# A three-mixer block with its input norm applied after the projections, and its bias table moved in pieces

## What is computed

```python
def rms_norm(x, w):
    y = x32 * lax.rsqrt(jnp.mean(x32 * x32, axis=-1, keepdims=True) + EPS)
    return (y * w.astype(f32)).astype(x.dtype)
...
h = rms_norm(x, norm1_w[l])
cols = split_cols(h @ w_in[l], IN_SIZES)
...
y_a = short_conv_mixer(a_b, a_c, a_u, conv_w[l], conv_b[l])    # b * (conv(c * u) + bias)
y_b = nsa_mixer(...)     # compressed, selected and window attention, with bias_w = rel_bias[t5_bucket(dist)]
y_c = mla_mixer(...)
y_d = stick_breaking_mixer(...)
x = x + rms_norm(y, ...) @ w_out[l]
```

## Time and profile before

| | |
|---|---|
| device time, three runs | 1957.11, 1959.37, 1961.04 us (median 1959.37) |
| span of the profiled execution | 1953.4 us |
| busy: PE / DVE / ACT / POOL | 1843.6 (94%) / 885.3 (45%) / 425.1 (22%) / 1018.2 (52%) us |
| weight slots | 284 of 512 KB, 3.3 us from issue to landing (median) |
| TensorE's granted clock, mean of the span | 0.970 of full |

### The profile page before, as it was taken

One profiled execution on the slowest core, in us unless ns is written; L12 is line 12 of the kernel. 1 busy time (PEld: TensorE's weight loads), 2 busy tenths in 40 slices (PEclk: granted clock), 3 DMA queues, 4 the chain that ended last, 5 costly groups with the idle time before them and its releaser, 6 DMA issues.

```text
span 1953.4 us, 21963 instructions
## 1 busy us (share of the span) xinstructions
PE 1843.6 (94%) x8480; PEld 1442.8 (74%) x8480; DVE 885.3 (45%) x1372; ACT 425.1 (22%) x910; POOL 1018.2 (52%) x584
## 2 busy tenths in 40 slices
PE   6699889999999999999999999999999899999996
PEld 4485556788888886777887778677778668888885
DVE  5236864664036322435004365666655654304434
ACT  1214565121012101222003132455400210000001
POOL 3492110566666665455664444444466646666664
PEclk8899999999999999999999889999999999999998
DMA  4441010222222223122322112311122212222221
GB/s 158 150 149 48 23 44 22 87 94 96 98 95 97 96 93 108 65 75 76 106 96 76 65 55 67 115 61 65 63 89 95 86 55 97 97 97 97 97 97 54
DMA packets 48526, 166.38 MB, mean 85 GB/s; under 512 B 5531, under 2 KB 6875, under 8 KB 48040
## 3 DMA queue, kind: packets, MB, share of 16 engines
q1 hardware_dynamic: 45596, 159.77, 24.4%
q10 hardware_dynamic: 2828, 5.21, 0.9%
HBM read 161.98 MB, written 3.94 MB: 85 GB/s over the span
## 4 chain that ended last, share of the span: by engine, by line
PE 79%; DVE 9%; POOL 3%; ACT 3%; issue 3%; DMA 3%; SPq 1%; DVEq 0%; ACTq 0%; POOLq 0%
PE bank L652 78%; DMA w_raw<-in_w 2%; POOL w_lo_t L1889 2%; DVE tmp L1404 2%; POOL w_hi_t L1887 1%; PE bank L910 1%; DVE o_hi L1382 1%; DVE o_lo L1383 1%; DVE att_l_t L1672 0%; DMA x_sb<-in_x 0%; ACT L1065 0%; DVE h_lo L1450 0%; ACT rstd_t L1114 0%; DVE att_l_t L1813 0%; SPq L1911 0%
## 5 line engine op out<-in xcount | busy, mean ns | idle before, releaser
L1887 POOL TENSOR_SCALAR w_hi_t<-w_raw 128x1024 fp32r<-128x1024 f32 x284 | 307.5, 1083 | 887.3 <-PE bank L652 835.3
L1889 POOL TENSOR_TENSOR w_lo_t<-w_raw,w_hi_t 128x1024 fp32r<-128x1024 f32 x284 | 693.1, 2440 | 23.7
L652 PE MATMUL bank<-h_hi,w_hi_t 128*128 128x512 f32 x1344 | 546.9, 407 | 25.8 <-POOL w_lo_t L1889 14.4
L652 PE MATMUL bank<-h_lo,w_hi_t 128*128 128x512 f32 x1344 | 531.0, 395 | 0.6 <-DVE h_lo L1450 0.5
L652 PE MATMUL bank<-h_hi,w_lo_t 128*128 128x512 f32 x1344 | 530.0, 394 | 0.0
L652 PEld LDWEIGHTS bank<-h_hi,w_hi_t 128*128 128x128 f32 x1344 | 256.6, 191 | 103.4 <-issue 31.1
L652 PEld LDWEIGHTS bank<-h_lo,w_hi_t 128*128 128x128 f32 x1344 | 256.9, 191 | 56.7 <-DVE h_lo L1450 3.6
L652 PEld LDWEIGHTS bank<-h_hi,w_lo_t 128*128 128x128 f32 x1344 | 256.5, 191 | 55.4 <-issue 0.2
L652 PE MATMUL bank<-hid_hi,w_lo_t 128*128 128x512 f32 x432 | 168.1, 389 | 0.0
L652 PE MATMUL bank<-hid_hi,w_hi_t 128*128 128x512 f32 x432 | 168.0, 389 | 0.0
L652 PE MATMUL bank<-hid_lo,w_hi_t 128*128 128x512 f32 x432 | 168.0, 389 | 0.0
(11 more groups left out here) (253 smaller groups left out, 2262.5 us busy)
## 6 DMA issues: line engine op xcount, KB each, us to landing
w_raw<-in_w SPq DMA_DIRECT2D x284, 512.0 KB, 3.3
x_sb<-in_x SPq DMA_DIRECT2D x4, 512.0 KB, 6.6
x_sb<-in_x ACTq DMA_DIRECT2D x2, 1024.0 KB, 5.6
alibi<-in_alibi SPq DMA_DIRECT2D x8, 256.0 KB, 5.9
out_y<-x_sb SPq DMA_DIRECT2D x8, 256.0 KB, 2.0
scratch<-table SPq DMA_DIRECT2D x1, 1280.0 KB
toep<-scratch SPq DMA_DIRECT2D x4, 256.0 KB
decay<-in_decay SPq DMA_DIRECT2D x1, 1024.0 KB, 4.9
```

The source lines that it names most:

```text
L652: return pe.matmul(out, lhs, rhs, start=start, stop=stop, **kw)
L1887: pool.tensor_scalar(hi, raw, 1.0, 0.0, ALU.mult, ALU.add).then_inc(*did("w_hi", i))
L1889: pool.tensor_tensor(lo, raw, hi.bitcast(F32), ALU.subtract).then_inc(*did("w_lo", i))
```

## The change

The factor r is kept in a buffer of its own, `r_h`, and is no longer in h: h_hi = rounded x * w (ACT, a new step "u"), h_lo = x * w - h_hi (DVE, one instruction of three operands). PE starts with kvc and ksw, two projections together, up to the last chunk but one; then the norm's sums, then the last chunk. nq0 follows on its own. Each evacuation multiplies by r_h on DVE; v1, which has positions on partitions, is scaled on ACT by a column `r_col` that PE makes by four small matmuls (step `r_cols`). In the convolution, b, c and u each need r: c is multiplied by r_h twice (for u too), and the sum that b multiplies once.

SP loads the first two weight slots ahead of x. `ones` and `ones64` are made by memsets on DVE and not loaded. Six weights and two masks of the mixers are loaded by ACT later, next to projections. The bias table is made after nq0, leaves at n = 6, goes to the scratch area head by head (n = 8 to 11) and comes back head by head (n = 13 to 16). `onehot`, `tab`, `causal` and `kv_raw` take other places in SBUF.

```diff
-    run(sqs("n1", KD) + [("norm", "n1"), ("apply_h", "n1", "norm1"), ("bias_tables", 0)])
-    part, ends = together(("kvc", "ksw", "nq0"))
-    run([part(0, KD)] + ends)
+    for c in range(KD):
+        run([("u", "n1", c), ("sq", "n1", c)])
+    part, ends = together(("kvc", "ksw"))
+    run([part(0, KD - 1), ("norm", "n1"), part(KD - 1, KD)] + ends)
...
-    run([("sq", "ksw", 0), F("nq1"), ("sq", "nq0", 0), ("norm", "ksw"), ("cmp_x", 0), ("nsa_apply", "ksw"),
-         F("cq0"), ("sq", "nq1", 0), ("norm", "nq0"), ("cmp_x", 1), ("nsa_apply", "nq0"),
+    run([("sq", "ksw", 0), ("cmp_x", 0), F("nq0"), ("cmp_x", 1), ("bias_tables", 0), ("norm", "ksw"),
+         ("nsa_apply", "ksw"), F("nq1"), ("sq", "nq0", 0), F("cq0"), ("sq", "nq1", 0), ("norm", "nq0"),
+         ("nsa_apply", "nq0"),
...
-         U(1, 0), F("sk0"), U(1, 1), F("sk1"), U(1, 2), v1[0], U(1, 3), v1[1], v1[2],
+         U(1, 0), F("sk0"), ("r_cols", "n1"), U(1, 1), F("sk1"), U(1, 2), v1[0], U(1, 3), v1[1], v1[2],
...
+UNNORMED = ("n1",)
+FIRST_LOADS = 2
+TABLE_AT, SCRATCH_AT, BIAS_AT = 6, 8, 13
...
+            elif stage == "u":
+
+                _, key, c = step
+                srcs, waits = norms[key][0], norms[key][6]
+                wait_src(act, waits[c])
+                act.activation(h_hi[:, c], srcs[c], ACT.Copy, scale=col(U_WEIGHT[key], c))\
+                   .then_inc(*did("h_hi", key, c))
...
+            elif stage == "u":
+
+                _, key, c = step
+                own("h_hi", key, c)
+                dve.scalar_tensor_tensor(out=h_lo[:, c], in0=norms[key][0][c], scalar=col(U_WEIGHT[key], c),
+                                         in1=h_hi[:, c].bitcast(F32), op0=ALU.mult, op1=ALU.subtract)\
+                   .then_inc(*did("h_ready", key, c))
...
+                elif name in ("ksw", "nq0", "nq1", "cq0", "ckv", "sk0", "sk1"):
+                    dst = {"ksw": ks_d, "nq0": nq[:, 0], "nq1": nq[:, 1], "cq0": cq[:, 0], "ckv": ckv[:],
+                           "sk0": s_qk[:, 2], "sk1": s_qk[:, 3]}[name]
+                    dve.wait_ge(*full(name))
+                    dve.tensor_tensor(dst, ps(name)[:], r_h[:], ALU.mult).then_inc(*release(name))
...
-                        ins = dve.tensor_copy(conv_t[:, 1, 2:2 + T], ps(name)[:])
+                        chain(dve.tensor_tensor(conv_t[:, 1, 2:2 + T], ps(name)[:], r_h[:], ALU.mult))
+                        ins = dve.tensor_tensor(conv_t[:, 1, 2:2 + T], conv_t[:, 1, 2:2 + T], r_h[:], ALU.mult)
...
+                        chain(dve.tensor_tensor(yc, yc, r_h[:], ALU.mult))
                         ins = dve.tensor_tensor(conv_t[:, 1, 2:2 + T], ps(name)[:], yc, ALU.mult)
...
+        def rows_of(h):
+
+            sp.wait_ge(C.sem["table_out"], 16)
+            for k, (c0, w) in enumerate(((0, 640), (640, 1024))):
+                rows = P if k == 0 else N_CMP
+                dst = a["scratch"][h, k, 0:rows * w].rearrange("(p w) -> p w", w=w)
+                sp.dma_start(dst, a["table"][h:h + 1, c0:c0 + w].to_broadcast([rows, w]))\
+                  .then_inc(C.sem["bias_out0"], 16)
+
+        def bias_of(h):
+
+            sp.wait_ge(C.sem["bias_out0"], 16 * 2 * NH)
```

More of the change, by code:

```diff
@@ L358, in _program @@
     epst = sb("epst", [P, 8])
+    r_h = sb("r_h", [P, T])
+    r_col = sb("r_col", [P, NT])
     area = ExitStack()
@@ L405, in _program @@
     ckv = sp_("ckv", [P, T])
-    sp_("rest of onehot", [P, 640 + 1024 - 1536])
+    sp_("up to cb_t", [P, 640 + 1024 - 1536])
     mq = sp_("mq", [P, NH, T])
@@ L554, in _program @@
     norm_at = {k: i for i, k in enumerate(norm_order)}
+    ring_order = [k for k in norm_order if k not in UNNORMED]
+    ring_at = {k: i for i, k in enumerate(ring_order)}
     sq_use = {}
@@ L710, in _ @@
                 ms(step[1], len(norms[step[1]][0]))
+            elif stage == "r_cols":
+                key = step[1]
+                pe.wait_ge(*after("rstd", key))
+                out = take(("r_cols", key))
+                for t in range(NT):
+                    last = mm(out[:, t:t + 1], r_h[0:1, t * P:(t + 1) * P], ones[0:1, 0:1], True, True,
+                              skip_group_check=True)
+                fill(("r_cols", key), last)
             elif stage == "sq" and step[1] in PE_SUM:
@@ L1408, in _ @@
         ins.then_inc(*did("table", "eps"))
+        dve.memset(ones[:], 1.0).then_inc(*did("ones_set"))
+        chain(dve.memset(ones64[:], 0.0))
+        for g in range(2):
+            gs = slice(g * HD, (g + 1) * HD)
+            chain(dve.memset(ones64[gs, gs], 1.0))
         dve.memset(rb[N_BUCKETS:N_BUCKETS + 1, :], NEG).then_inc(*did("bcast_v"))
@@ L1894, in _ @@
     def _(sp):
+        for i in range(FIRST_LOADS):
+            sp.dma_start(w_raw[:, i], a["w"][i]).then_inc(C.sem[f"w_landed{i}"], 16)
         for g in range(4):
@@ L1897, in _ @@
         n = 0
-        def bias_tables(part):
-            if part == 0:
-                for nn in range(len(TAB)):
-                    sp.wait_ge(*evacuated(("tab", nn)))
-                sp.dma_start(a["table"], tab[:]).then_inc(C.sem["table_out"], 16)
-                return
-            if part == 1:
-                sp.wait_ge(C.sem["table_out"], 16)
-                for k, (c0, w) in enumerate(((0, 640), (640, 1024))):
-                    rows = P if k == 0 else N_CMP
-                    dst = a["scratch"][:, k, 0:rows * w].rearrange("h (p w) -> h p w", w=w)
-                    sp.dma_start(dst, a["table"][:, None, c0:c0 + w].to_broadcast([NH, rows, w]))\
-                      .then_inc(C.sem["bias_out0"], 16)
-                return
-            sp.wait_ge(C.sem["bias_out0"], 16 * 2)
-            t = a["scratch"].tensor
-            for h in range(NH):
-                sp.dma_start(toep[:, h], bass.AP(tensor=t, offset=(2 * h) * P * 1024 + P - 1,
-                                                 ap=[[640 - 1, P], [1, T]])).then_inc(C.sem["bias_in"], 16)
-                sp.dma_start(cb_t[:, h], bass.AP(tensor=t, offset=(2 * h + 1) * P * 1024 + T - CMP_LEN + 1,
-                                                 ap=[[1024 - CMP_STRIDE, N_CMP], [1, T]]))\
-                  .then_inc(C.sem["bias_in"], 16)
@@ new lines, in table_to_dram @@
+        def table_to_dram():
+            for nn in range(len(TAB)):
+                sp.wait_ge(*evacuated(("tab", nn)))
+            sp.dma_start(a["table"], tab[:]).then_inc(C.sem["table_out"], 16)
+        def rows_of(h):
[5 more added lines that the diff above has]
+                  .then_inc(C.sem["bias_out0"], 16)
```

128 lines of the change are left out of this document (77 added, 51 removed).

## The result

The changed kernel is slower: 1966.01 us median (1961.55 to 1967.24, 8 runs) against 1958.01 (1954.91 to 1961.04, 8 runs), a ratio of 1.0035, 95% interval 1.0024 to 1.0045. The forecast was 1953.8. The profiled execution has a span of 1965.0 us against 1953.4; these are 11.6 apart where the medians are 8.0 apart, because the profiled execution of the kernel before was its shortest run.

The account below looks back on a forecast made before the run. PE's matmuls were taken to bound the kernel, with only idle time before 151 us movable: 9.7 us gained at slot 16 minus 4.1 in the convolution, 5.6 off, gave 1953.8 us (own range 1950 to 1956.5; 8 in 10: 1934 to 1964).

Parts of the forecast that it names:

- the change touches none of those after the first mixer: PE's matmuls, nearly all of the 1953.4 us, stay untouched after the first mixer; only idle time before 151 us can move.
- The start: Up to the third weight slot: weights ahead of x, no wait for the norm; third slot done at 34.1, 9 us early.
- The bytes on one engine: Table to slot 16: scratch pieces, bias reads, weights and ACT's loads on one DMA engine at 25 GB/s, 52.3 us.
- the sum's 0.7 us of an idle engine: Ahead of slot 16: 0.7 us counted where the bias reads wait for the last scratch write.
- What waits beside POOL: DVE instructions reading two SBUF tensors wait while POOL works: 2.82 us beside it, 0.74 alone.
- The allowance of 3.4 us: First compress input on DVE: two-SBUF forms meet POOL's slot 5, up to 3.4 us more, making the table later.
- From span to time: Last step: median of the runs lies 6 us over the profiled span, so span 1947.8 becomes 1953.8 us.
- The rule for the rows: DMA copies: engines are the largest number up to 16 dividing the slowest dimension, so 31 rows run on one engine.
- The convolution's term: Four additional DVE multiplies by r_h in the convolution, on the chain: 4.1 us lost, between 1 and 6.
- Evacuations at nothing: Ten evacuation copies move from ACT to DVE multiplies of PSUM by r_h: taken as nothing, at most 10 x 0.1 us.
- Rival B: Slower: the queue stands at each of eight pieces; at 1.5 us each 12 us lost, 1966 us; chance 0.18.
- Rival A: Pieces nearly free: 31-row DRAM-to-DRAM copies spread, 1.1 us each; slot 16 at 91 to 93, 1936 us; chance 0.17.

Follow-up runs that it names:

- a_col: Changed kernel with r_col kept in unused columns of epst, so the working area starts at a multiple of 128 bytes again; 1954.3 us, ratio 0.9987 to before.
- b_pad: Kernel before with 32 unused bytes behind epst, so its working area starts at 32 modulo 64; 1966.41 us, ratio 1.0051.
- a_rows32: Changed kernel with 32 unused bytes behind r_col and its 31-row transfers made 32 rows; 1941.28 us, ratio 0.9914 to before.
- a_pad: Changed kernel with 32 unused bytes behind r_col, so the working area starts at 64 modulo 128; 1957.67 us, ratio 0.9997 to before.
- a_w32: Changed kernel with 32 unused bytes ahead of w_hi_t, so the split weights start at 32 modulo 64; 1977.2 us, ratio 1.0101 to before.

## Why the prediction was wrong

- **The step that failed** is the first paragraph's "the change touches none of those after the first mixer", and with it that nothing later is changed. The instructions and their order are the same there, but their operands' addresses are not: 9.4 us between the changed kernel and a_col, 10.0 between before and b_pad. None of the rivals held it. The 9.4 us are nearly the whole distance from the forecast's upper edge, 1956.5, to 1966.01.
- **The start was right.** First split 4.54 (5.5), slots 0 and 1 done at 11.8 (13.4), DVE's last h_lo at 22.95 (25.5), table copies at 46.1 (47.4), slot 16 at 109.0 (109.8), v1 9.9 us early (9.7). The bytes on one engine were right too, as the 32 rows show: from the table's landing to slot 16's 57.0 us (forecast 56.6). SyncE stood 8.5 us at the first bias read, but this isn't the sum's 0.7 us of an idle engine: the one engine worked on at 25 to 33 GB/s until the last scratch piece was written. That the sum met the trace within 1 us is in part luck, since it kept the one engine busy without a gap, and the chain has 11.3 us of POOL's splitting (82.79 to 94.07) between two loads.
- **What waits beside POOL** was drawn too narrowly, as instructions with two SBUF inputs. In the first compress input it was also a cast with one, 2.44 us beside POOL and 0.43 in the second input:

```profile
35.63 2.44 DVE L1408 CAST cmp_xh<-tmp 128x512 fp32r<-128x512 f32 x1
...
41.32 0.43 DVE L1408 CAST cmp_xh<-tmp 128x512 fp32r<-128x512 f32 x1
```

The allowance of 3.4 us held it all the same: that input took 6.1 us (32.72 to 38.81), forecast 2.8 + 3.4.
- **From span to time** the forecast added 6 us "for what lies around it". In the changed kernel's profiled run that is 1.8 us (1966.75 and 1965.0); the rest was that the profiled execution of before was the shortest of its runs. Against the eight runs' median of 1958.01, 5.6 us off would be 1952.4.
- **The rule for the rows.** The Trainium skill, "DMA: Bandwidth & Descriptors", section "Why a DMA increments its semaphore by 16 and not by 1", says that a copy runs on the largest number of engines up to 16 that divides the slowest dimension of both its sides. The trace agrees for a copy from DRAM to DRAM too: 25 GB/s with 31 rows, over 300 with 32.
- **The convolution's term was too small**: 4.1 against 4.7 to 5.3 in the traces up to 256 us and 6.1 to 9.2 in medians. (ac, 0) took 2.17 us, and the forecast had 1.9 to 2.1 for it. What is missing isn't shown; a lower clock behind PE's longer pauses would fit.
- **Evacuations at nothing** isn't contradicted: the 10 multiplies lie before v1, where the sum came out. No run tested it by itself.
- With the address put back (a_col) the change gives -2.5 us of the forecast -5.6, within 0.2% of the kernel before: 9.9 to 10.7 gained at the start, 5 to 9 given back by the four multiplies.
- Rival B named the right time, 1966, for a wrong reason: the start came out as forecast, and the issues of pieces take 1.2 us of the chain (48.45 to 49.73), where B needed 12. Rival A wasn't this kernel, but it is a_rows32: 16.2 us for it, where A had 17.8 more than the forecast.

## What to carry to other kernels

When a change adds, drops or resizes a tensor, compare the start addresses of all matmul operands before and after, and keep them at multiples of 128 bytes, which was the fastest of the starts tried here; a tensor of 16 bytes below a working area cost this kernel 0.5%. A group whose mean grows by a few ns in a stage that the diff doesn't touch, at full clock and 100% busy, is the mark of it. Give transfers a row count that divides over the engines even if the last row is waste, and fold a factor into an instruction that is there anyway before adding one on the chain.

## What the runs showed of the hardware

- Back-to-back fp32r matmuls of 512 columns start every 226.7 ns if both operands start at a multiple of 128 bytes in the partition (before, a_col), every 228.9 on average if the moving one starts at 64 modulo 128 (a_pad), and every 233.3 if the moving (b_pad) or the stationary one (a_w32) starts at 32 modulo 64 and the other doesn't. Other offsets, both at 32, and a stationary operand at 64 modulo 128 weren't tried. The weight loads of hid's matmuls take 187 to 188 ns in all cases.
- VectorE didn't feel the shift in the one form compared: the 512-column multiply from PSUM into conv_t took 0.69 us in a_col and in the changed kernel.
- A VectorE cast of one SBUF tensor took 2.44 us beside GpSimd's split and 0.43 alone (changed kernel, 35.63 and 41.32 us).
- A 31-row transfer occupies one DMA engine also from DRAM to DRAM (25 GB/s in the changed kernel before the first read into cb_t); a 32nd row that nothing uses, in these and in the reads, took 16.2 us off a kernel of 1958.
